# Differential layer: three quarters of four output panels multiplied in the last head's steps

## What is computed

```python
def diff_attention(q, k, v, lam):
    def block(qb):
        s = jnp.einsum('bqhjd,bkhjd->bhjqk', qb, k).astype(jnp.float32) * scale
        p = jax.nn.softmax(s, axis=-1)
        a = (p[:, :, 0] - lam * p[:, :, 1]).astype(v.dtype)
        return jnp.einsum('bhqk,bkhe->bqhe', a, v)
    return map_query_blocks(block, q)

def diff_out(o, z, subln_g, lam_init, w_out):
    o = rms_norm(o, subln_g) * (1.0 - lam_init)
    return gated_out(o, z, w_out)          # (o * silu(z)) @ w_out

xp = xp + gt_p * op
xs = xs + gt_s * os_
```

## Time and profile before

| | us |
|---|---|
| median of 3 runs | 2177.76 |
| lowest, highest | 2173.09, 2180.71 |
| the profiled execution, its own time | 2180.25 |
| its span in the trace | 2178.5 |
| step 35 to the end of step 39, within the span | 819.8 to 861.4 |
| the eight output panels with their adds | 861.4 to 925.1 |

### The profile page before, as it was taken

One profiled execution on the slowest core, in us unless ns is written; L12 is line 12 of the kernel. 1 busy time (PEld: TensorE's weight loads), 2 busy tenths in 40 slices (PEclk: granted clock), 3 DMA queues, 4 the chain that ended last, 5 costly groups with the idle time before them and its releaser, 6 DMA issues.

```text
span 2178.5 us, 35475 instructions
## 1 busy us (share of the span) xinstructions
PE 2021.1 (93%) x14168; PEld 1742.8 (80%) x14168; DVE 1114.4 (51%) x2333; ACT 803.8 (37%) x1824; POOL 653.9 (30%) x884
## 2 busy tenths in 40 slices
PE   6999999989999997969979999999998889999997
PEld 4788888878988895968956868688787878888887
DVE  5476675663454453476544234242152365776764
ACT  5355564233444343031132232223321024655542
POOL 1233222542444322435410110201212654232332
PEclk8899999989999998979979999999999889999999
DMA  9112213412232223134222334324245322011111
GB/s 342 51 47 80 62 41 91 137 49 82 79 93 73 64 66 112 44 53 155 88 63 73 88 107 120 108 73 113 82 141 100 104 75 60 4 51 53 41 40 49
DMA packets 302865, 182.60 MB, mean 84 GB/s; under 512 B 59621, under 2 KB 276974, under 8 KB 302702
## 3 DMA queue, kind: packets, MB, share of 16 engines
q1 hardware_dynamic: 284436, 159.44, 25.1%
q10 hardware_dynamic: 18266, 20.90, 3.9%
HBM read 154.56 MB, written 25.74 MB: 83 GB/s over the span
## 4 chain that ended last, share of the span: by engine, by line
PE 77%; DVE 8%; ACT 7%; DMA 4%; issue 2%; SPq 1%; ACTq 1%; POOL 0%; DVEq 0%; POOLq 0%
PE pc L1713 21%; PE acc L1639 10%; PE acc L728 6%; PE acc L1835 4%; PE acc L1824 4%; PE pc L783 3%; PE acc L718 3%; PE pt L1846 3%; PE pt L728 3%; PE acc L2076 2%; PE acc L2088 2%; DMA out_mlstm_n<-amat 1%; PE acc L672 1%; PE acc L1667 1%; PE pt L2096 1%
## 5 line engine op out<-in xcount | busy, mean ns | idle before, releaser
L1549 POOL TENSOR_TENSOR idle<-eps 128x1 f32<-128x1 f32 x146 | 43.5, 298 | 1458.8 <-PE pc L783 297.5
L1553 POOL TENSOR_TENSOR wl<-raw,wh 128x256 fp32r<-128x256 f32 x584 | 467.2, 831 | 11.7
L1713 PE MATMUL pc<-hh,wh 128*128 128x320 f32 x1152 | 381.0, 331 | 15.8 <-DVE hl L2743 7.7
L1713 PE MATMUL pc<-hl,wh 128*128 128x320 f32 x1152 | 363.0, 315 | 0.0
L1713 PE MATMUL pc<-hh,wl 128*128 128x320 f32 x1152 | 362.8, 315 | 0.0
L1713 PEld LDWEIGHTS pc<-hh,wh 128*128 128x128 f32 x1152 | 222.5, 193 | 28.0 <-issue 16.2
L1713 PEld LDWEIGHTS pc<-hl,wh 128*128 128x128 f32 x1152 | 223.7, 194 | 0.2 <-issue 0.2
L1713 PEld LDWEIGHTS pc<-hh,wl 128*128 128x128 f32 x1152 | 222.7, 193 | 0.0
L1550 POOL CAST wh<-raw 128x1024 fp32r<-128x1024 f32 x146 | 152.8, 1047 | 0.3
L2367 ACT COPY ht<-pt 128x512 f32<-128x512 f32 (+1 forms) x160 | 76.2, 525 | 191.3 <-PE pt L1846 191.3
L2850 DVE TENSOR_REDUCE gst<-acc 128x1 f32<-128x640 f32 (+1 forms) x160 | 113.3, 708 | 2.8 <-PE acc L1824 2.6
(11 more groups left out here) (399 smaller groups left out, 4428.2 us busy)
## 6 DMA issues: line engine op xcount, KB each, us to landing
raw<-in_w_mod SPq DMA_DIRECT2D x144, 256.0 KB, 3.4
raw<-in_gqa_w_in SPq DMA_DIRECT2D x80, 256.0 KB, 3.5
raw<-in_diff_w_in SPq DMA_DIRECT2D x64, 256.0 KB, 3.7
raw<-in_mlstm_w_in SPq DMA_DIRECT2D x64, 256.0 KB, 3.3
raw<-in_gqa_w_out SPq DMA_DIRECT2D x36, 256.0 KB, 3.3
praw<-in_w_mod SPq DMA_DIRECT2D x32, 256.0 KB, 9.6
out_mlstm_C<-amat ACTq DMA_DIRECT2D x16, 512.0 KB, 7.1
raw<-in_mlstm_w_out SPq DMA_DIRECT2D x32, 256.0 KB, 3.2
```

Source lines behind the costliest of these rows:

```text
L1553: ins = pool.tensor_tensor(wl[:, s, k:k + 2], raw[:, r, k:k + 2], wh[:, s, k:k + 2].bitcast(F32), ALU.subtract)
L1713: ins = pe.matmul(pc[:, c:c + 320], w[:, sl, kt, :], h[:, kt, t:t + 320], start=kt == 0 and n == 0, stop=kt == KT - 1 and n == 2)
```

## The change

In the differential layer, three quarters (blocks 0 to 5, that is heads 0 to 5) of output panels 0 to 3 are multiplied in steps 35 to 38, one whole panel of 36 matmuls a step, at the end of the step's list on PE. DVE adds each result to x one step later on, behind its `combine`. What is left of these four panels, blocks 6 and 7, is packed by SP as one panel (`rest_item`) and multiplied after output panel 4, 12 matmuls for each. Then panels 5, 6 and 7 follow as before. The number of matmuls stays the same. SP's and POOL's order of panels is changed accordingly. Beside that the first split slots of layers 0 and 1 are 2 and 1 instead of 0 and 2, which only turns the numbers of the three slots around. The rest of the diff moves helpers so that both kinds of layer can call them, and removes the differential layer's own ending.

```diff
@@ out_slots
-            if kind == "diff":
-                return [((s + i) % SPL, (i,)) for i in range(KT)]
-            return [((s + EARLY + i) % SPL, panels) for i, panels in enumerate(GQ_OUT)]
+            return [((s + EARLY + i) % SPL, panels) for i, panels in enumerate(OUT)]
...
-        FIRST_SLOT = (0, 2, 0, 2)
+        FIRST_SLOT = (2, 1, 0, 2)
         EARLY, EARLY_KT = 4, 6
...
@@ SP
+                def rest_item(wo):
+
+                    slot = ring()
+                    panel(slot, [(raw[:, slot, 4 * k:4 * k + 4, :],
+                                  wo[(EARLY_KT + k) * P:(EARLY_KT + k + 1) * P, 0:EARLY * P].rearrange("p (i c) -> p i c", c=P))
+                                 for k in range(2)], [w_full[wring()]] * RAW)
...
-                            for m in range(16, 22):
-                                mod_item(m)
-                            item(wo, 0)
-                            mod_item(22)
-                            mod_item(23)
-                            item(wo, P)
+                            for m, i in ((16, 0), (None, 1), (18, 2), (20, 3), (22, None)):
+                                if i is None:
+                                    item(wo, EARLY * P)
+                                if m is not None:
+                                    mod_item(m)
+                                    mod_item(m + 1)
+                                if i is not None:
+                                    item(wo, i * P)
+                            rest_item(wo)
...
-                for i in range(2 if kind == "diff" else EARLY + 1, KT):
+                for i in range(EARLY + 1, KT):
...
@@ POOL
+                            if i is not None:
+                                split(ring(), wring(), [early_done] * SPL, 2)
+                    split(ring(), wring(), proj_done, EARLY)
...
@@ PE
+            def early_open():
+
+                seen(raw_full[ring()], 32)
+                early_slot[0] = wring()
+                pe.wait_ge(*seen(w_full[early_slot[0]]))
+                pe.wait_ge(*seen.at(y_ready, EARLY_KT))
...
-                if kinds[layer] == "diff":
-                    for sl in outs_open[1:-1]:
-                        project(sl, yh, yl, freed_by=x_ready)
-                    last_panel(outs_open[-1], yh, yl)
-                    outs_open.clear()
-                    return
...
                     if qt == 3:
                         token_major(h + 1) if h + 1 < NH else mods_summed(20, 21)
+                    if h + 1 == NH and qt < EARLY:
+                        early_open()
+                        for half in range(2):
+                            for _ in early_mms(half):
+                                pass
...
@@ DVE, diff_layer
                     if n + 1 < NN:
                         combine(n + 1)
+                    if last and qt:
+                        for half in range(2):
+                            early_gated(1, qt - 1, half)
                 output(NN - 1)
...
-                if kind == "gqa":
-                    dve.wait_ge(*seen(early_added, 2 * EARLY))
+                dve.wait_ge(*seen(early_added, 2 * EARLY))
```

More of the change, by code:

```diff
@@ L426, in build @@
         PANELS = {"gqa": 5 * GQ_KV, "diff": 4 * NH}
-        FIRST_SLOT = (0, 2, 0, 2)
+        FIRST_SLOT = (2, 1, 0, 2)
         EARLY, EARLY_KT = 4, 6
-        GQ_OUT = ((4,), (0, 1, 2, 3), (5,), (6,), (7,))
-        LAST_ORDER = [i for panels in GQ_OUT for i in panels]
+        OUT = ((4,), (0, 1, 2, 3), (5,), (6,), (7,))
+        LAST_ORDER = [i for panels in OUT for i in panels]
         def totals(kind, layer):
@@ L1596, in _ @@
                         mod_item()
[L1597 to L1603, removed]
+                    for m, i in ((16, 0), (None, 1), (18, 2), (20, 3), (22, None)):
+                        if i is None:
+                            split(ring(), wring())
+                        if m is not None:
+                            mod_item()
+                            mod_item()
+                        if i is not None:
+                            split(ring(), wring(), [early_done] * SPL, 2)
+                    split(ring(), wring(), proj_done, EARLY)
+                for i in range(EARLY + 1, KT):
                     split(ring(), wring())
@@ L1989, in attention_out @@
                 final = layer + 1 == DEPTH
-                for i in range(2 if kinds[layer] == "diff" else EARLY + 1, KT):
+                for i in range(EARLY + 1, KT):
                     out_panel()
@@ L2773, in normalise, with early_gated @@
                 seen(h_ready, 4)
+            def early_gated(layer, i, half):
+                (t, c), mod = HALF[half], mods[layer % 2]
+                dve.wait_ge(*seen(early_done))
+                for a0, a1, g in (((0, P, 0), (P, 320, 1)), ((0, 320, 1),))[half]:
+                    ins = dve.scalar_tensor_tensor(out=x[:, i, t + a0:t + a1], in0=pc[:, c + a0:c + a1], scalar=mod[:, 2 * KT + i, g:g + 1],
+                                                   in1=x[:, i, t + a0:t + a1], op0=ALU.mult, op1=ALU.add)
+                ins.then_inc(early_added, 1)
             def minus(out, a, high):
@@ L2790, in gate @@
                                              op0=ALU.add, op1=ALU.mult).then_inc(c_free[half], 1)
[L2792 to L2799, removed]
                 def k_reciprocal(j):
@@ L2899, in gqa_layer @@
                     if n and early_at(n - 1) is not None:
-                        early_gated(*early_at(n - 1))
+                        early_gated(layer, *early_at(n - 1))
                     if st == 1 and g:
@@ L2926, in gqa_layer @@
                 y_low(NN // QT - 1)
-                early_gated(*early_at(NN - 1))
+                early_gated(layer, *early_at(NN - 1))
                 seen.end(totals("gqa", layer))
```

## The result

The changed kernel takes 2187.61 us (median of 8 runs, 2182.98 to 2194.39), the kernel before 2176.98 us (8 runs, 2173.09 to 2180.71): 10.6 us more, ratio 1.004 with a 95% interval of 1.0028 to 1.0052. The predicted time was 2188.0. Its profiled execution took 2184.47 us, with a span of 2182.7.

A forecast was written before the change was run, and what follows sets the result against it. TensorE was taken as the bound, busy 93% of the span. The 21.1 us leaving the output panels return as longer steps (0.0), plus 10.4 us of clock loss: 2190.7 us profiled, 2188.0 against the median, range 2176 to 2197.

The forecast's parts named there:

- idle time ahead of panel 0: Step 35: PE waits 4.7 us for panel 0's weights to be transferred and split, starting the panel at 829.5 us.
- sums' end to step 36: Step 35: idle time of 4.7 us, then panel 0's 5.3 us; step 36 starts 8.8 us later than now.
- step 36: Last head: round plus early panel takes 13.8 us, with shorter context-tile values but ACT's table load of 1.2 us.
- step 37: Last head: 14.8 us, as DVE's `y_low`, which waits for ACT, stands ahead of the combine; early panel strung on.
- step 38: Last head: scores 3.0, to combine's end 4.45, first add 0.66 and panel 5.3 make 13.4 us, against 6.1 today.
- step 39: Last head: waits for modulation weights go, leaving 5.7 us against 10.7 now; output panels start at 882.5 us.
- output panels to the last add: Output stage after step 39: loses 144 matmuls, 21.1 us; the wait for head 7's y stays.
- loss by the clock in four bursts: Early panels 0 to 3: each burst starts at half clock after idle time, losing 2.6 us, 10.4 us in all.
- The sum: Whole kernel: 2180.25 + 0.0 + 10.4 = 2190.7 us for the profiled execution, 2188 against the median of 2177.76.
- (a): Early panels: clock stays at 2.4 GHz or is soon back; 2178 us, or 2184 with four cheap falls; chance 0.23.
- (b): Steps 36 to 38: adds aren't what panels wait for; panels fill idle time, 7.4 us less, 2170 us; chance 0.07.
- (c): Step 36 or 37: output panel weights late behind modulation panels in SP's queue; +6 more, 2194 us; chance 0.10.

The follow-up runs named there:

- e5: The changed kernel unchanged, timed and profiled again; 2191.81 us, ratio 1.0043 to the kernel before.
- e2: Changed kernel with DVE's three adds of an early panel moved from behind the next step's combine to ahead of its maxima; 2180.60 us, ratio 0.9997 to before.
- e4: As e3, but with DVE's adds back at the end of the step, behind the combine; 2184.99 us, ratio 1.0016 to the kernel before.
- e6: Changed kernel with 30 added filler matmuls in step 35, in PE's idle time ahead of panel 0; 2190.29 us, ratio 1.0037 to the kernel before.
- e3: As e2, with the early panels also one step later (steps 36 to 39), ahead of turn and modulation sums; 2170.10 us, ratio 0.9944 to before.
- e7: e3 with 7 and 10 added filler matmuls in two gaps between step 35's sums and step 36's columns; 2165.05 us, ratio 0.9925 to the kernel before.
- e1: Kernel before with only the first slots of layers 0 and 1 changed to 2 and 1; 2183.51 us, ratio 1.0003 to the kernel before.

## Why the prediction was right

The sum was made for the profiled execution, so I set its terms against the profile after. Start is the end of the sums of step 35 (824.83 before, 818.92 after).

| | predicted, us | measured, us |
|---|---|---|
| idle time ahead of panel 0 | 4.7 | 4.73 |
| sums' end to step 36, at full clock | 10.0 | 12.62 - 2.78 = 9.8 |
| step 36, at full clock | 13.8 | 15.16 - 1.53 = 13.6 |
| step 37, at full clock | 14.8 | 16.44 - 2.04 = 14.4 |
| step 38, at full clock | 13.4 | 16.01 - 2.90 = 13.1 |
| step 39 | 5.7 | 5.6 |
| output panels to the last add | 63.7 - 21.1 = 42.6 | 926.70 - 884.75 = 42.0 |
| loss by the clock in four bursts | 10.4 | 9.2 (e5: 10.2) |

**The steps.** Right. Each of the early panels 1 to 3 was strung onto the round of scores, maxima, exponentials and combine instead of filling its idle time. e2 shows the adds' place as the cause: with nothing moved but the adds, the 10 us are gone; e4 shows it once more from the other side. Both take away or bring back waits and falls of the clock together. What the falls alone cost is read from the lengths of the bursts, and only for panel 0 does a run (e6) change the idle time by itself.

**The clock.** Right in mechanism and nearly in size. The idle stretches were predicted as 4.7, about 5, 4.4 and 2.6 us and are 4.73, 2.71 + 2.34 with the turn of 0.76 between, 4.17 and 2.53. All four are followed by a stretch at half clock. The loss of 2.6 us a burst was a choice between two rows, 1.5 and 7.2; measured are 1.5 to 2.9, and 1.8 to 3.0 in e5. What the Trainium skill says on the page "TensorE: Matmul & The Clock Gate", section "HAM oscillation — how this bites in real kernels", of bursts parted by waits agrees with it, by the four bursts in two executions and by the filled one in e6.

**The sum** was 2.9 us too high for this execution (+10.4 against +7.5 in the layer): 1.2 by the clock, 1.2 by steps a little shorter than worked out, 0.6 in the output panels. Of these 0.6 some 0.5 are the first panel: before the change its 42 matmuls began at half clock, behind values of 2.50 us, and took 6.7 us; now they take 6.3. The medians give +10.6 and +9.9, 2 to 3 us more than the layer; where these lie isn't shown. That the median came out within 0.4 us of the forecast is therefore partly luck: the sum's own terms are 2.9 us off in the profile for which it was made.

**The rivals.** (a), a kept clock, is refuted by both profiles of the changed kernel. (b), the panel filling the idle time, doesn't happen in the changed kernel, but it is what e3 does: 0.994. The price put on it (7.4 us less than before; its own steps, 13.8 + 14.8 + 13.4 against 3 x 11.4, give 7.8) was about half to two thirds of what e3 gives, since e3 also removes the wait of step 35. (c), late weights, didn't happen in the changed kernel, with room as stated (5.2 us for panel 3); it did in e2, by 4.87 us. From the page "SBUF — State Buffer" of the Trainium skill the prediction allowed up to 3 us for instructions of DVE and POOL that exclude each other. In the profiled execution of the changed kernel the combines of steps 37 to 39 were not held (0.89 us each). Held were instructions off the path: the combine of step 36 (1.31 us at 821.02, while PE waited for weights) and L2999 (1.37 us against 0.82 in its next call). e6 shows 0.9 us of it on the path.

## What to carry to other kernels

Work that is moved into the idle time of an engine stays free only if nothing it waits for sits behind the loop's own round: give the instruction that frees its buffer a place at the head of the other engine's step, where its operands are already there, not at the tail. Put such work a step after its operands' transfers could be asked for, and check the next wait in the queue, which the first one may have hidden. On TensorE count an idle stretch of the size seen here, 2.5 us and more, twice, once as idle time and once as the slow start behind it; the slow start may stay out in one execution and come in the next, as below for head 7's y. The short ones cost little beyond themselves: behind 0.50 and 0.88 us of waiting (e3, e7) the burst was 0.3 us longer.

## What the runs showed of the hardware

A burst of 36 matmuls behind idle stretches of 2.5 to 5.2 us lost 1.5 to 3.0 us to the half clock, in 8 of 8 cases in two executions of the changed kernel, and 0.3 us with the stretch filled down to 0.82. It surprised me that 2.63 to 2.71 us of idle time, 0.77 us of transposes and another 2.34 to 2.41 are no better than one piece of 4.2: panel 1 lost 1.5 us in one execution and 3.0 in the other. So one profile tells the price of such a stretch only to about 1.5 us.

The wait for head 7's y, behind 42 dense matmuls and five transposes, is 2.59 to 2.82 us in every profile, and yet the clock fell behind it in six of nine (before, after, e1, e4, e6 and e7) and not in e2, e3 and e5. It isn't the longer waits that brought the fall: e3 kept its clock behind 2.79 us, the kernel before lost it behind 2.59. A fall costs 1.5 us there. So two executions of one kernel can differ by that much in the layer, and bursts and steps tell more than the layer's sum alone.

A DVE instruction of one column with two operands (0.22 us) took 0.70, and the combine of 640 columns (0.89) took 1.31, while POOL's split ran beside them. The page "SBUF — State Buffer" of the Trainium skill, section "SBUF: two separate sides", says that such pairs exclude each other; the waits here, 0.5 and 0.4 us, are shorter than one piece of the split, 3.35 / 4 = 0.84 us.
